# ScalarE copies the next block's rows behind both sigmoids, and VectorE turns them last

## The reference

```
def expert_block(args):              # 'lax.map' over blocks of rows, each of one expert
    toks, e = args
    xb = x_pad[toks]                                  # rows of 1024
    hb = jax.nn.silu(xb @ w1[e]) * (xb @ w3[e])       # w1, w3: 1024 x 512
    return hb @ w2[e]                                 # w2: 512 x 1024
```

## Time and profile before

| | us |
|---|---|
| median of 3 runs | 3134.55 |
| lowest, highest | 3132.65, 3138.47 |
| the profiled execution | 3157.24 |
| its span, first to last instruction | 3155.8 |
| TensorE busy in the span | 2642.2 (84%) |
| VectorE busy | 1365.3 (43%) |
| ScalarE busy | 1051.0 (33%) |
| GpSimd busy | 647.3 (21%) |

### The profile page before, as it was taken

One profiled execution on the slowest core, in us unless ns is written; L12 is line 12 of the kernel. 1 busy time (PEld: TensorE's weight loads), 2 busy tenths in 40 slices (PEclk: granted clock), 3 DMA queues, 4 the chain that ended last, 5 costly groups with the idle time before them and its releaser, 6 DMA issues. The chain is left out here.

```text
span 3155.8 us, 63798 instructions
## 1 busy us (share of the span) xinstructions
PE 2642.2 (84%) x23589; PEld 1368.9 (43%) x23589; DVE 1365.3 (43%) x2816; ACT 1051.0 (33%) x1942; POOL 647.3 (21%) x914
## 2 busy tenths in 40 slices
PE   7999999968898989999999927977678846777777
PEld 3444444424454444454355514544344423443443
DVE  2141424237787878888677721211111111111118
ACT  2313030216777777777222112111111111111114
POOL 0101010110121111111022222322232212222233
PEclk8999999988999999999999959988899878898889
DMA  8020201175776776767434365566455587656537
GB/s 300 13 80 15 78 27 67 49 258 179 264 252 225 238 235 228 247 223 240 157 126 144 120 244 194 191 208 240 152 198 174 165 294 245 237 156 246 186 107 305
DMA packets 225280, 576.76 MB, mean 183 GB/s; under 512 B 78230, under 2 KB 94679, under 8 KB 208780
## 3 DMA queue, kind: packets, MB, share of 16 engines
q1 hardware_dynamic: 123304, 427.99, 37.7%
q0 software_dynamic: 101440, 145.99, 15.4%
q10 hardware_dynamic: 324, 0.10, 0.0%
HBM read 460.86 MB, written 112.29 MB: 182 GB/s over the span
## 5 line engine op out<-in xcount | busy, mean ns | idle before, releaser
L2000 PE MATMUL bank<-w,hT 128*32 128x256 f32 x5120 | 348.2, 431 | 315.2 <-DVE hT L2037 315.2
L2033 DVE TENSOR_TENSOR sg<-sg,bank 128x128 f32<-128x128 f32 x160 | 44.6, 279 | 978.9 <-ACT sg L1970 978.7
L1253 DVE TENSOR_TENSOR_SCAN left<-leave,left 128x512 f32<-128x512 f32 (+3 forms) x320 | 358.4, 1120 | 135.9 <-ACT leave L1135 135.3
L2000 PEld LDWEIGHTS bank<-w,hT 128*32 128x32 f32 x5120 | 173.0, 124 | 483.3 <-DVE hT L2037 347.9
L442 PE MATMUL bank<-xnT,w_in 128*128 128x512 f32 x768 | 330.3, 592 | 0.0
L1944 POOL DMA_DIRECT2D ys_d<-y x164 | 115.9, 712 | 810.0 <-issue 743.6
L1056 POOL DMA_DIRECT2D w_out<-in_cache_v x256 | 137.8, 538 | 661.2 <-issue 656.0
L1965 ACT ACTIVATE o_rs<-rowsP 128x512 f32 (+1 forms) x81 | 92.9, 1146 | 464.6 <-DMA rowsP<-xs_d 454.2
L1935 POOL DMA_DIRECT2D rowsP<-xs_d x324 | 215.1, 672 | 85.1 <-issue 84.2
L1993 PE MATMUL bank<-w,o_sq 128*32 128x256 f32 x3840 | 214.7, 382 | 20.0 <-DVE o_sq L2028 20.0
L1620 PE MATMUL bank<-w_out,w 128*128 128x512 f32 x512 | 229.4, 601 | 2.5 <-DVE w L1684 2.5
(11 more groups left out here) (409 smaller groups left out, 3424.9 us busy)
## 6 DMA issues: line engine op xcount, KB each, us to landing
w<-in_w SPq DMA_DIRECT2D x54, 2048.0 KB, 15.9
w_out<-in_cache_v POOLq DMA_DIRECT2D x256, 256.0 KB
w_out<-in_cache_k SPq DMA_DIRECT2D x256, 256.0 KB
oT<-in_w SPq DMA_DIRECT2D x22, 2048.0 KB, 14.1
w_out<-in_w SPq DMA_DIRECT2D x20, 2048.0 KB, 14.4
ys_d<-zeros SPq DMA_DIRECT2D x32, 816.0 KB
ys_d<-y POOLq DMA_DIRECT2D x166, 128.0 KB, 4.8
rowsP<-xs_d POOLq DMA_DIRECT2D x324, 64.0 KB, 4.0
```

Of the source, the lines that this page charges most:

```text
L1253: dve.tensor_tensor_scan(left[n % 4][:, 0:cols][:, ::-1], leave[n % 4][:, 0:cols][:, ::-1], leave[n % 4][:, 0:cols][:, ::-1], left[n % 4][ ...
L2000: mm = pe.matmul(yb[q * Q:q * Q + Q, u * (XW // 2):(u + 1) * (XW // 2)], hT[:, u, j, :], w2[i][:, j, q * (XW // 2):(q + 1) * (XW // 2)], s ...
```

## The change

In ScalarE's body the call `landed(n + 1)`, which waits for the next block's rows and copies them, moves from ahead of the two calls of `gated` to behind them. In VectorE's body the two calls of `turn_rows(n + 1, u)` move out of the loop over the units, behind both. Nothing else is changed: the same instructions, buffers and semaphores, and the weights' DMAs are issued in the same form.

```diff
         def body(n, e, b, extra):
-            landed(n + 1)
             for u in range(UNITS):
                 gated(n, u)
+            landed(n + 1)
             result(n)
...
                 dve.drain()
                 dve.transpose(hT[:, u, :, :].rearrange("p j b -> p (j b)"), hid[:, u, :].rearrange("p (a j) -> p j a", j=EC)).then_inc(s["hT"], 1)
+            for u in range(UNITS):
                 turn_rows(n + 1, u)
```

## The result

| | before | after |
|---|---|---|
| median | 3134.84 | 3197.72 |
| lowest, highest | 3132.65, 3138.47 | 3196.90, 3199.09 |
| the profiled execution | 3157.24 | 3199.09 |
| first hidden step of the stage | 1846.5 | 1847.7 |
| end of the last out product | 3058.6 | 3103.0 |

Times are in us, 4 runs of each; the profiled execution of before is a fifth one. The ratio is 1.020, with an interval of 1.0182 to 1.0218: the change makes the kernel **slower by 63 us**. The direction was predicted; 3170 was 28 us too low.

The account below looks back on a forecast made before the run. The prediction took weight bursts and the row loads' timing against them to bound the experts' stage; +36.3, +5 and -6.2 summed to +35 us on the median 3134.55, giving 3170, with an overall range of 3095 to 3203.

Parts of the forecast that it names:

- What bounds it, and where the wait goes: Experts' stage: weight bursts and row loads bound it; TensorE's 315.2 us wait moves from out product to hidden step.
- The lock: Experts' stage: one late row load makes the next late, burst after burst; every burst catches a load, chance 0.60.
- B + 22.8: Late rows' copy on ScalarE, claimed 22.8 us after B, the time SP issues a burst of weights.
- c + 11.1: SP's next burst after c, the copy of late rows; forecast at c + 11.0 for an expert of two blocks.
- the rival by which some loads escape: GpSimd's row loads at bursts: several issued early enough to escape, giving 3060 to 3128 us; chance 0.17.
- interval of two blocks: Time between SP's bursts for an expert of two blocks: 33.8 us, and 10.42 more for each further block.
- 22 intervals against 862.7: Burst intervals outside the six experts taken apart: 899.0 us where they took 862.7 before, +36.3 us.
- six experts apart, against 156.6: Six experts around those of one block: 151.0 us (-5.6) to +16 against 156.6; +5 taken.
- first burst, against 1921.90: Start of the experts' stage: SP's first burst at 1915.7 where it was at 1921.90, -6.2 us.
- behind the last burst, to the end of the stage: After the last burst: both orders stall once, and once by the loads of x1; 0, within 8 us.
- the base: Final step: +35 us added to the median 3134.55 for 3170; against the profiled execution the sum gave 3192.
- The rival by the rule: Experts' stage: rows land when they landed before, so the gain stays; 3000 us, chance 0.11.

Follow-up runs that it names:

- e4: Against the kernel before: only VectorE's two turns moved last, ScalarE's order as before; 3146.87 us (0.999).
- e9: Against the changed kernel: GpSimd stores a result before it waits for its row load's landing; 3051.81 us (0.969 of the kernel before).
- e5: Against the changed kernel: w1, w3 and w2 each loaded by four DMAs in runs of 4 KB, same bytes; 3058.90 us (0.973 of the kernel before).
- e6: Against the kernel before: w1, w3 and w2 loaded in the same 4 KB runs, old order kept; 3062.95 us (0.974).
- e8: Against the changed kernel: SP's w1 and w3 wait for the hidden step one block further on; 3202.19 us (1.019 of the kernel before).

## Why the prediction was right in direction and 28 us low

**What bounds it, and where the wait goes: right.** The wait at L2000 fell away and returned before the hidden step. It is found 29 times, as predicted, but the count is in part luck: 23 are plain ones, of 10.5 us on average (10 to 11 were predicted), and the other six are those of the start, the one-block experts and `x1`. From late copy to hidden step 1.65 us; the slow clock costs 2.35 us on average where 2.1 were taken.

**The lock: right, and stronger than its own numbers.** Late copies were taken at B + 22.8; the 23 plain ones average 22.7. The next load was to come 1.9, 0.6 and -0.7 us behind the burst for two, three and four blocks; it comes 1.2 to 2.9, 0.3 to 2.2 and 0.1 to 2.6 behind. The burst comes at c + 11.1, as predicted; GpSimd's loop is slower than I had put together from rows: 3.40 us from store to the next expert's load where 3.03 were taken (2105.63 to 2109.03), 2.14 for 1.93 (2116.12 to 2118.26). So not even the experts of four blocks come near to escaping, and the rival by which some loads escape (0.17) fell.

**The sum, step by step**, against the profiled execution of before:

| | predicted | measured |
|---|---|---|
| interval of two blocks | 33.8 | 33.2 to 34.4 |
| three, four blocks | 44.2, 54.6 | 43.8 to 45.1, 54.7 to 55.1 |
| 22 intervals against 862.7 | +36.3 | 902.2: +39.4 |
| six experts apart, against 156.6 | +5 | 161.1: +4.5 |
| first burst, against 1921.90 | -6.2 | 1915.84: -6.1 |
| behind the last burst, to the end of the stage | 0, within 8 | +6.5 |
| behind the stage | none | -2.7 |
| profiled execution | +35 | +41.9 |

All terms hold within their bounds. The +5 for the six experts was a middle value between -5.6 and +16, and for the 7.3 us behind the +16 no row is given; the copies at the three pairs came 33.4, 37.0 and 38.0 us behind the first burst of each, between the 32.4 that were taken and 39.7. That the term fits so well is partly luck. The largest miss is the one that I had not worked out: behind the last burst (2941.21 to 3058.6 before, 2979.12 to 3103.0 after) the loads of `x1` make TensorE wait twice in the changed order (4.40 and 4.42 us, each with a slow hidden step of 8.80 behind it) and once in the old one (5.69 us).

**The step that failed is the last one, the base.** In the prediction's words, "against it the sum gives 3192, and against the median 3134.55 + 35 = **3170**". The +35 was worked out for one execution of before, 22.7 us slower than the median. I treated these 22.7 us as something that both kernels have. But the sum replaces the stage of before, with all its stalls, by an absolute pattern: every burst catches one load. Such a pattern has no much faster or slower executions, and it doesn't become 22.7 us shorter because the median of another kernel is. So 3192 was the number to predict, and 41.9 + 22.7 - 1.4 = 63.2 is what was measured against 3134.55. The runs bear this out: after varies by 2.2 us in 4 runs, the kernel before by 24.6 us in its five executions beside it, the profiled one included, and by 40 us on one of the chips (3133.77 to 3173.39 in 19 runs). Nor can the 22.7 us lie mainly outside the stage. In the 14 profiles it begins at 1843.2 to 1853.1, 1846.5 in that of before, and from its end to the end of the span it is 94.5 to 97.2 us. What makes the old order's stage longer or shorter from run to run stays open. That it is the count of caught loads is not shown: before's profile has 14 of them and e4's 13, with 25.6 us of wait between them, and the kernel before has only one trace.

**The rival by the rule.** The rule of the Trainium skill quoted in the prediction ("DMA: Bandwidth & Descriptors", "Rules for kernel authors": issue early, wait late) would have given 3000. (That price takes 2.9 us for the slow hidden step; with the 2.1 us of the sum it would be about 20 us lower.) The trace disagrees for this kernel alone (3197.72), and agrees once GpSimd's own wait for the landing is moved behind its store too (e9, 3051.81 against 3072.79 of the old order). It is a rule on one wait; two waits of different engines on the same landing have to be moved together.

**Where the expectation of e5 and e6 failed.** I had taken the price of a caught load to shrink with the length of a packet, to about a quarter. Each turn did shrink, from 0.62 to 0.22 us, but the number of turns that the load has to wait rose from some 27, where the burst ended, to all of its own 54. The Trainium skill ("DMA: Bandwidth & Descriptors", section "Queues, rings and completion order") has an engine take turns between queues too, but with a whole packet of some 9 to 17 descriptors in each. The trace doesn't agree for the weights' queue: one run of 16 KB is one of the trace's packets, and between 2086 and 2098 each of the 310 packets of weights starts directly behind one of the rows' queue. With nine such runs a turn, eight of nine would start behind another packet of weights.

## What to carry to other kernels

Before moving a wait on one engine, write down what the engine behind it releases, at which distance behind the late event, and set that beside the next self-timed event of every other engine: here 11.1 us for the burst against 13.4 us for the load decided most of the 63 us. Where two periodic streams can lock, ask which of them is to be early, and give it that by its own engine's order (here GpSimd's store ahead of its wait) before taking stalls away from the other. And where the changed kernel is predicted as an absolute pattern, compare it as an absolute time with the median; a difference worked out against a profiled execution may be carried over only if both kernels repeat it.

## What the runs showed of the hardware

A load of 0.26 MB, copied 6.3 us behind its first issue when it is alone, is copied 19 to 23 us behind it when issued beside 6.29 MB in runs of 16 KB (the queues' turns of 0.62 us, until the burst ends), and mostly 15 to 17 us beside the same bytes in runs of 4 KB (0.22 us, all 54 turns). The load and the store beside it take 54 turns an engine though only 8 of them carry 4 KB; the others are packets under 512 bytes. The shorter runs don't come free: SP needs 4.45 + 2.15 us to issue a burst instead of 0.82 + 0.33, and the weights' queue takes more of the DMA engines' time for the same bytes. The queue in the page of after and of e5 (packets, MB, share of 16 engines' span of 3197.5 and 3058.5 us):

```profile
q1 hardware_dynamic: 123304, 427.99, 37.3%
```

```profile
q1 hardware_dynamic: 163912, 428.01, 41.2%
```

That is 1193 and 1260 us of all 16 engines, 67 us more. I had not expected, either, that TensorE is at the 1.2 GHz level (granted clock 0.50) behind a stall of 7.23 us (9.16 us for the hidden step of 2131.30 in e5), nor that a kernel can be steadier and slower at once: the locked order repeats within 0.1% (after, 4 runs) and 0.3% (e8, 4 runs), the free one within 0.8% in its five executions beside after and 1.3% in 19 on another chip.
